# Experts' places dealt out by rank, a values' stage that takes two row tiles ahead of its weights, and block loops that end at the count

## What is computed

```python
expert = g_idx[:, None] * MOE_PER_GROUP + top_i          # two experts per token
def block_ffn(args):
    e, idx = args
    xb = h_pad[idx]
    return (jax.nn.silu(xb @ w1[e]) * (xb @ w3[e])) @ w2[e]   # 1024 -> 512 -> 1024
...
z = h @ w_in                                             # GLA: q, k, v, gate, low ranks
```

## Time and profile before

| | us |
|---|---|
| median of 3 runs | 2832.69 (2831.58 to 2833.03) |
| profiled execution, its own time | 2834.07 |
| its span, first to last instruction | 2832.3 |

### The profile page before, as it was taken

One profiled execution on the slowest core, in us unless ns is written; L12 is line 12 of the kernel. 1 busy time (PEld: TensorE's weight loads), 2 busy tenths in 40 slices (PEclk: granted clock), 3 DMA queues, 4 the chain that ended last, 5 costly groups with the idle time before them and its releaser, 6 DMA issues. The chain is left out here.

```text
span 2832.3 us, 62953 instructions
## 1 busy us (share of the span) xinstructions
PE 2289.7 (81%) x24871; PEld 1539.8 (54%) x24872; DVE 1249.3 (44%) x2297; ACT 741.5 (26%) x1653; POOL 393.1 (14%) x592
## 2 busy tenths in 40 slices
PE   6888780895699999986619998979688399999895
PEld 3667670784355555543317885758577255554452
DVE  4779999666222222221135401328565422222224
ACT  5210101551121222211134312448532022111112
POOL 1000001000111111110012100025300111111112
PEclk9889895896899999988759999989898699999998
DMA  8374342235935557999955311014553999999994
GB/s 320 105 238 133 122 149 82 78 112 212 405 133 214 219 218 277 358 408 409 399 198 192 127 52 46 23 43 164 207 194 129 406 396 407 408 408 408 407 368 185
DMA packets 228379, 662.92 MB, mean 234 GB/s; under 512 B 26125, under 2 KB 56925, under 8 KB 228247
## 3 DMA queue, kind: packets, MB, share of 16 engines
q1 hardware_dynamic: 196028, 576.63, 53.5%
q0 software_dynamic: 19280, 56.60, 5.6%
q10 hardware_dynamic: 12940, 27.91, 3.0%
HBM read 583.52 MB, written 77.55 MB: 233 GB/s over the span
## 5 line engine op out<-in xcount | busy, mean ns | idle before, releaser
L1533 PE MATMUL moe_pg<-feed_w,moe_xt 128*32 128x256 f32 x11200 | 673.2, 394 | 107.3 <-SPq L1467 96.0
L1533 PEld LDWEIGHTS moe_pg<-feed_w,moe_xt 128*32 128x32 f32 x11200 | 357.5, 113 | 363.1 <-SPq L1467 100.1
L1526 PE MATMUL moe_py<-feed_w,moe_at 128*32 128x256 f32 x5536 | 334.8, 382 | 0.0
L1648 DVE TENSOR_TENSOR moe_a<-moe_sil,moe_pg 128x128 f32<-128x128 f32 x175 | 50.4, 288 | 644.3 <-ACT moe_sil L1606 644.3
L1640 DVE COPY moe_y<-moe_py 32x256 f32<-32x256 f32 x346 | 146.9, 424 | 283.6 <-PE moe_py L1526 278.2
L1606 ACT ACTIVATE moe_sil<-moe_pg 128x128 f32<-128x128 f32 x175 | 48.5, 277 | 701.6 <-PE moe_pg L1533 701.6
L1526 PEld LDWEIGHTS moe_py<-feed_w,moe_at 128*32 128x32 f32 x5536 | 161.6, 109 | 110.9
L1492 POOL COPY moe_idx<-plan_token 128x1 int32 (+1 forms) x183 | 33.5, 183 | 1273.0 <-DVE moe_x_rows L1636 872.3
L1592 ACT ACTIVATE moe_y<-moe_py 32x256 f32<-32x256 f32 x346 | 129.0, 373 | 279.1 <-PE moe_py L1526 274.9
L1495 POOL DMA_INDIRECT moe_xg<-scratch_experts_in,moe_idx x183 | 178.7, 977 | 144.1 <-POOL moe_idx L1492 144.1
L104 PE MATMUL taps_zg<-ht_conv_hi,taps_w_hi 128*128 128x512 f32 (+1 forms) x192 | 77.6, 404 | 66.3 <-DVE taps_w_lo L549 51.6
(11 more groups left out here) (356 smaller groups left out, 3922.7 us busy)
## 6 DMA issues: line engine op xcount, KB each, us to landing
feed_w<-in_moe_w SPq DMA_DIRECT2D x384, 1024.0 KB
taps_ada_w<-in_ada_w SPq DMA_DIRECT2D x40, 1024.0 KB, 7.0
scratch_experts_out<-moe_y ACTq DMA_DIRECT2D x175, 128.0 KB, 4.8
taps_raw<-in_conv_pw_w SPq DMA_DIRECT2D x20, 512.0 KB, 9.1
scan_v<-scratch_gla_values SPq DMA_DIRECT2D x20, 512.0 KB, 4.0
front_w<-in_ada_w SPq DMA_DIRECT2D x8, 1024.0 KB, 18.3
cv_raw<-in_gla_w_in SPq DMA_DIRECT2D x16, 512.0 KB
scratch_gla_out<-scan_o SPq DMA_DIRECT2D x16, 512.0 KB, 6.0
```

The lines of the kernel that those rows point to most:

```text
L1526: last = pe.matmul(out[j * BLK:(j + 1) * BLK, 0:CUT], at[:, c * BLK:(c + 1) * BLK], feed.back[:, buf, c, j * CUT:(j + 1) * CUT], start=c = ...
L1533: last = pe.matmul(pg[j * BLK:(j + 1) * BLK, 0:2 * P].rearrange("t (m n) -> t m n", m=2), xt[:, c % 2, (c // 2) * BLK:(c // 2 + 1) * BLK], ...
```

## The change

1. **Places.** Before, ranks 3 and up alternate: the largest, the smallest, the next largest, the next smallest and so on. After, ranks 3 to 30 are cut into four runs of seven; each group of four places takes one rank of each run, and the last rank comes last.
2. **Values' stage.** SP loads both first `x` tiles, waits for the second gathered row tile of tile 0 (`gathered10`), and only then issues the eight value pieces. ScalarE and VectorE work on tiles 0 and 1 between pieces 0 to 3; pieces 4 to 7 come next, and then tile 2. TensorE turns tile 1 before its first product.
3. **Loops.** The loop over blocks runs to the count in a register instead of to the most blocks possible.

```diff
-MIDDLE = 18
+LATER = ((7, -26.0), (14, -29.0), (21, -26.0), (28, -3.0))
...
                 link(dve.tensor_scalar(place, key, float(feed.AHEAD), 0.0, ALU.subtract, ALU.max))
-                link(dve.tensor_scalar(bend, key, -4.0, float(4 * MIDDLE - 3), ALU.mult, ALU.add))
-                link(dve.scalar_tensor_tensor(place, bend, 0.0, place, ALU.min, ALU.add))
-                link(dve.tensor_tensor(place, place, key, ALU.add))
+                for i, (at, shift) in enumerate(LATER):
+                    link(dve.tensor_scalar(bend[:, i, :], place, float(at), shift, ALU.is_ge, ALU.mult))
+                link(dve.tensor_reduce(numbered, bend.rearrange("p i e -> p e i"), AX.X, ALU.add))
+                link(dve.scalar_tensor_tensor(place, place, 4.0, numbered, ALU.mult, ALU.add))
+                link(dve.scalar_tensor_tensor(place, key, float(feed.AHEAD), place, ALU.min, ALU.add))
...
-            with eng.Fori(1, nb // UNROLL) as i:
+            with eng.Fori(1, (count + (UNROLL - 1)) >> 2) as i:
...
-                load_x(0)
-                for q in range(RB):
-                    load_w(q)
-                load_x(1)
-                for q in range(RB, 2 * PIECES):
+                for t in range(2):
+                    load_x(t)
+                sp.wait_ge(s("gathered10"), 16)
+                for q in range(2 * PIECES):
                     load_w(q)
...
                 turn(0)
+                turn(1)
                 product(V0, 0)
-                turn(1)
...
+                first(0)
+                first(1)
+                root(0)
+                highs(0)
+                scale(0)
+                highs(1)
+                root(1)
+                high(0)
+                scale(1)
+                highs(2, 3)
+                high(1)
+                for t in range(2, TILES + 1):
+                    if t == 2:
+                        highs(4, 5, 6, 7)
...
+                second(0)
+                rstd(0)
+                lows(0)
+                second(1)
+                modulate(0)
+                rstd(1)
+                lows(1)
+                low(0)
+                lows(2)
+                modulate(1)
+                lows(3)
+                low(1)
+                for t in range(2, TILES + 1):
+                    if t == 2:
+                        lows(4, 5, 6, 7)
```

More of the change, by code:

```diff
@@ L1090, in route @@
         place = sb([P, EXPERTS])
-        bend = sb([P, EXPERTS])
+        bend = sb([P, len(LATER), EXPERTS])
+        numbered = sb([P, EXPERTS])
         first_of = sb([P, EXPERTS])
@@ L1254, in _ @@
                                        numbers.unsqueeze(1).to_broadcast([1, EXPERTS, PER_GROUP, GROUPS]), ALU.mult))
-                link(dve.tensor_reduce(bend[0:1, :], by_place, AX.X, ALU.add))
-                dve.tensor_copy(plan.order[:, :], bend[0:1, :]).then_inc(s("told"), 1)
+                link(dve.tensor_reduce(numbered[0:1, :], by_place, AX.X, ALU.add))
+                dve.tensor_copy(plan.order[:, :], numbered[0:1, :]).then_inc(s("told"), 1)
                 dve.wait_ge(s("told"), 4)
@@ L1443, in blocks @@
                 body(k, 0, k)
-            with eng.Fori(1, nb // UNROLL) as i:
+            with eng.Fori(1, (count + (UNROLL - 1)) >> 2) as i:
+                i = nc.s_assert_within(i, 1, nb // UNROLL - 1,
+                                       skip_runtime_bounds_check_because="count is at most nb, a multiple of UNROLL")
                 for p in range(UNROLL):
@@ L1898, in result, with highs @@
                         .then_inc(s("out_ready"), 1)
-                for q in range(PIECES):
-                    w_high(q)
+                def highs(*pieces):
+                    for q in pieces:
+                        w_high(q)
                 first(0)
[L1903 to L1908, removed]
+                first(1)
[11 more added lines that the diff above has]
+                        highs(4, 5, 6, 7)
                     if t < TILES:
+                        first(t)
                         root(t)
-                    if t >= 1:
+                    if t >= 3:
                         high(t - 1)
@@ L1978, in _, with lows @@
                                              ALU.add, ALU.mult).then_inc(s("cols_ready"), 1)
-                for q in range(PIECES):
-                    w_low(q)
+                def lows(*pieces):
+                    for q in pieces:
+                        w_low(q)
                 dve.wait_ge(s("cols_ready"), 2)
-                for t in range(TILES + 1):
+                second(0)
[13 more added lines that the diff above has]
+                        lows(4, 5, 6, 7)
                     if t < TILES:
                         second(t)
[L1985 to L1988, removed]
+                    if t >= 3:
                         modulate(t - 1)
```

## The result

| | before | after |
|---|---|---|
| median of runs, us | 2832.33 (2831.58 to 2833.03, 4 runs) | 2781.66 (2777.26 to 2782.82, 4 runs) |
| span of the profiled execution, us | 2832.3 | 2779.7 |

The ratio of the times is 0.9817, with a 95% interval of 0.9803 to 0.983: faster by 50.7 us. Forecast were 2786.6 and 46.1 less, with a range of 2771 to 2808.

The account below looks back on a forecast made before the run. Layer 0 was taken as TensorE-bound, then weight-bound at its end, with SP's issues holding TensorE; layer 1 as transfer-bound. 29 + 4.6 + 7.5 + 5 = 46.1 us less gave 2788.0, median 2786.6; range 2771 to 2808.

Parts of the forecast that it names:

- Layer 0, places: Layer 0's experts: the new order of places shortens the stage by 29 us, bounds 22 and 38.
- The walk: Step-by-step reckoning of layer 0's 32 places with fixed prices; waits 72 us on the old order, 53 on the new.
- the 50 to 55 that the prediction named as its sign: Layer 0: TensorE's waits for SP would total 50 to 55 us; staying at 70 or vanishing would refute the prediction.
- the step that the prediction worked out in full: Layer 0, place 15: SP's last issue for place 17 ends at 36.7 us, so TensorE waits 8.2 us.
- the 3 us that were added for its small waits: Layer 0: half of the 6 us that the walk charges too much for small waits, added to the gain.
- Rival 1: SP's issues don't hold TensorE, only data counts: layer 0 gains 50, total 67, 2765.6 us; chance 0.08.
- rival 2: Weight stream binds from place 23, small waits grow: layer 0 gains 15, values' stage nothing, 2805.5 us; chance 0.17.
- Rival 3: Values' stage gets slower, pieces 4 to 7 delaying tile 2: 5 us lost, total gain 36, 2796.6; chance 0.15.
- Layer 1, places: Layer 1's transfer-bound experts: 6.15 us less at the last place, some 1.5 lost to an empty queue: 4.6 less.
- Routing: Longer routing chain, 1.0 us more per layer, hidden behind PE's 18.3 us wait for the identity's transfer: nothing paid.
- Loops: End of both experts' stages: ScalarE's last copy no longer waits for empty iterations, 3.9 and 3.6, 7.5 us less.
- Values' stage: First product 13 us earlier, tile 2's delay gives part back: 5 us less, bounds 2 more and 9 less.

## Why the prediction was right, and where its sizes were off

**Layer 0, places: right in mechanism, 29 for 35.7.** The walk's picture of the large waits holds. It foresaw 8.2 us at places 15, 19 and 23, 4.0 at 26, 8.1 at 27 and 1.3 at 29. The timeline of TensorE has waits at just these places, of 6.58, 6.00, 6.58, 3.88, 4.45 and 3.24 us (ahead of them stand places 3 and 7):

```profile
761.38 1.89 PE L1538 MATMUL moe_pg<-feed_w,moe_xt 128*32 128x256 f32 x26 [0.90 <-SPq L1472]
...
886.84 3.66 PE L1538 MATMUL moe_pg<-feed_w,moe_xt 128*32 128x256 f32 x64 [0.96 <-SPq L1472]
...
1093.13 6.53 PE L1538 MATMUL moe_pg<-feed_w,moe_xt 128*32 128x256 f32 x64 [6.58 <-SPq L1472]
...
1176.70 5.71 PE L1538 MATMUL moe_pg<-feed_w,moe_xt 128*32 128x256 f32 x64 [6.00 <-SPq L1472]
...
1260.04 5.01 PE L1538 MATMUL moe_pg<-feed_w,moe_xt 128*32 128x256 f32 x64 [6.58 <-SPq L1472]
...
1315.39 6.34 PE L1538 MATMUL moe_pg<-feed_w,moe_xt 128*32 128x256 f32 x64 [3.88 <-SPq L1472]
1328.73 6.49 PE L1538 MATMUL moe_pg<-feed_w,moe_xt 128*32 128x256 f32 x64 [4.45 <-SPq L1472]
...
1365.60 5.14 PE L1538 MATMUL moe_pg<-feed_w,moe_xt 128*32 128x256 f32 x64 [3.24 <-SPq L1472]
```

All fourteen waits come to 37.4 us, below the 50 to 55 that the prediction named as its sign. At place 3 it foresaw 5.6 us in both orders, and both traces have 0.90 (760.58 in the kernel before). So the walk's 72 us for 70.5 on the old order was in part luck: 4.7 too much there, some 3 too little elsewhere. In the difference of the two orders that error drops out.

SP's timeline ahead of place 15 shows the step that the prediction worked out in full:

```profile
1058.74 2.49 SPq L1026 DMA_DIRECT2D feed_w<-in_moe_w  x4
1067.04 0.89 SPq L1034 DMA_DIRECT2D feed_w<-in_moe_w  x2
1069.38 2.21 SPq L1026 DMA_DIRECT2D feed_w<-in_moe_w  x4
1074.06 4.98 SPq L1034 DMA_DIRECT2D feed_w<-in_moe_w  x2
1080.49 9.31 SPq L1026 DMA_DIRECT2D feed_w<-in_moe_w  x4
1089.89 3.13 SPq L1034 DMA_DIRECT2D feed_w<-in_moe_w  x2
```

Six issues into an empty queue, six more, then place 17's, which the queue holds up for 9.31 + 3.13 us. The last ends at 1093.02, and TensorE starts at 1093.13. From the walk's zero (1058.54, the end of place 11's last first half) that is 34.5 us, where the walk had 36.7. The mis-sized price is the depth of the queue. The view of the transfers (queue of SP, 1058.7 to 1093.02: packets, MB, share) has the bytes that had left by then:

```profile
q1 hardware_dynamic: 3116, 12.04, 89.2%
```

That is 11.5 of the eighteen transfers, so 6.5 were outstanding when the last issue ended, where the walk had 5.4. The same count gives 6.6 to 6.8 at the ends that released places 19, 23 and 27, and 5.4 to 6.0 at the ends of the other stretched issues: the depth is not one number, and the walk took the lower one for the steps that count. Between the walk's own results for 5.4 (29 less) and 7 (38 less), 6.5 gives 35. That is an estimate; the depth was not varied by itself.

Two more terms were off, in opposite directions. The waits fell by 33.1 us (70.5 to 37.4), where the walk had 19, or 22 with the 3 us that were added for its small waits. The restarts after them gave back 3.0 us, where 7 were counted: waits over 2 us for weights fell from eight to six, not from 11 to 7, and the 64 matmuls behind them took 16.7 us more than 3.59 each in all before, and 13.7 after. A single one takes 5.01 to 6.53 us, so 1.4 to 2.9 more, instead of the 1.76 of the earlier trace rows.

**Rival 1 was wrong, though its price is near what SP's issues hide.** Its price, layer 0 gaining 50, assumed that SP's issues don't matter. They do, and when they are taken out of both kernels the places are worth 58 us. The prediction's sentence "TensorE waits for issues, not only for data" holds for the new order; for the old order's tail the data were as late as the issues.

**Rivals 2 and 3.** The stream of rival 2 does bind at the end of layer 0: with direct waits, the four waits that remain all lie from 1285.69 on. But the small waits before them did not grow (0.80 to 0.96 us each), and layer 0 gained 35.7 and not 15. Rival 3 is out: the values' stage got shorter in every trace with its new order.

**Layer 1, places: 4.6 for 5.5.** The transfers remain the bound, as forecast (DMA share 1.01). But 13.3 us more can be had from the same transfers, as the run without SP in between shows, and the forecast did not see them. The bytes of SP's queue tell where. The stage's 192 transfers of weights and the identity are 201.4 MB. The kernel after has moved them from 2151 to 2699, the one with direct waits from 2128.5 to 2679 (queue of SP: packets, MB, share), and there TensorE's last wait for weights ends at 2678.90:

```profile
q1 hardware_dynamic: 52697, 201.42, 92.3%
```

```profile
q1 hardware_dynamic: 52695, 201.40, 92.0%
...
2678.90 6.24 PE L1538 MATMUL moe_pg<-feed_w,moe_xt 128*32 128x256 f32 x64 [3.77 <-DMA feed_w<-in_moe_w]
```

Counted from SP's first issue for weights (2151.04 and 2128.56) the stream takes about 548 us in one and 550 in the other. TensorE ends at 2726.6 and at 2690.8, so 28 us behind the stream's end with SP's count and 12 us behind it with direct waits. So it is not the stream that got shorter; TensorE no longer trails it by the blocks that SP's late news had held back. (The queue stays busy for another 14 us in both, with rows that the next step needs.) The same count in the kernel before gives 547 and 34 us. The new places thus took 6 us off what trails and put 1 us on the stream, which is the forecast's mechanism at nearly its sizes (6.15 and 1.5). The count takes the queue's bytes in the order of issue, so its ends are good to a microsecond or so.

**Routing: nothing paid, as said.** Its start to the first activation of layer 1 takes 61.2 us instead of 60.7, and TensorE's wait for the identity, 15.6 us in layer 0 where it was 18.3, still covers the longer chain. The seven steps take 1.73 us where the three took 0.67, so 1.06 more; 1.0 was forecast.

**Loops: 7.5 for 7.4.** Both copies start 0.2 us behind TensorE's end, which answers to the earlier trace rows:

```profile
1386.76 1.93 PE L1531 MATMUL moe_py_last<-feed_w,moe_at 128*32 128x256 f32 x32 [1.16 <-DVE moe_at L1662]
...
1388.88 0.77 ACT L1597 ACTIVATE moe_y<-moe_py_last 32x256 f32<-32x256 f32 x2 [2.63 <-PE moe_py_last L1531]
...
2724.70 1.93 PE L1531 MATMUL moe_py_last<-feed_w,moe_at 128*32 128x256 f32 x32 [1.16 <-DVE moe_at L1662]
...
2726.83 0.77 ACT L1597 ACTIVATE moe_y<-moe_py_last 32x256 f32<-32x256 f32 x2 [2.62 <-PE moe_py_last L1531]
```

**Values' stage: 5 for 2.7.** The start came as forecast: 28.4 us from the stage's first transfer to the first product, where 28 were worked out and the earlier trace rows have 40.8. The give-back was mis-sized. "Tile 2 is added at 1491, scaled at 1494" put its turn 52.5 us after the first transfer; it came after 56.0. The step that failed is that only the pieces were followed to tile 2: the gate's rows stand behind two other transfers in SP's program, as the run with the gate's rows ahead shows, and moving them returned 3.0 of the 3.5 us. The stage is only 2.3 us short of its forecast; where the rest of the 3.5 came back was not traced.

The forecasts of the loops and of the places in layer 1 were right to a microsecond. The layer 0 term was 6.7 short and the values' term 2.3 long, so part of the total's agreement is luck: the two errors have opposite signs, and 3 us at the kernel's end are scatter.

## What to carry to other kernels

When a trace names a go-between (here the engine that issues transfers) for every wait, ask whether the data behind it had landed: on the old order 66 of 70 us stayed when the go-between was removed, on the new one the same edit gave 25 us. Let the consumer wait for the transfer's own semaphore when the engine that passes the news on also issues large transfers. A small transfer that the next step needs (the gate's rows) is late by everything that its queue's program waits for ahead of it, so list every input of a step before moving the large ones.

## What the runs showed that I had not expected

- Taking SP out of the handover saved 13.3 us in layer 1 in each of two kernels, although the DMA share is 1.02 with and without it (2250 to 2730, on the old places). In a stage bound by transfers, the work that trails behind the last one is still open to saving.
- The 64 matmuls of a half block take 3.59 to 3.66 us in the flow of blocks, and in the kernel after 5.01 to 6.53 us after an idle time of 3 to 7 us. The windows around the wait at place 15 in the kernel after show the granted clock falling while TensorE idles and staying low through these matmuls:

```profile
1076.00:1086.00 10.00, 10.00 (x169) 5.45 (x161) 1.91 (x6) 2.07 (x6) 2.13 (x3) 1.00 1.02 408
1086.00:1093.00 7.00, 0.55 (x9) 0.14 (x1) 1.34 (x4) 0.75 (x2) 1.16 (x2) 0.70 1.03 411
1093.00:1099.50 6.50, 6.37 (x64) 2.88 (x64) 0.00 (x0) 0.00 (x0) 0.00 (x0) 0.54 1.02 404
1099.50:1106.00 6.50, 6.50 (x105) 3.63 (x101) 1.63 (x5) 1.53 (x5) 1.16 (x2) 1.00 1.03 411
```

  At 0.54, close to the lower level of 1.2 GHz, they take 6.53 us; from 1099.5 on the clock is 1.00 again. A wait thus costs its own length and up to 2.9 us more.
- A loop whose end is in a register kept a block's beat of 6.15 us, and the skipped iterations, four with sixteen bodies, had cost ScalarE 6.5 us. The Trainium skill ("Runtime: NRT & Kernel Launch", Instruction fetch mechanics) names a stall for a taken branch whose target lies outside the instructions held at the time; both loops take one per iteration, and no run here shows its price.
